# Relative-bias rows: 32 copies per head in eight stores and shifted loads in four pieces, in place of 128 copies in one store

## The reference

```
bucket = t5_bucket(max(t - s, 0))             # 32 buckets of distance
bias   = rel_bias[bucket]                     # [32 buckets, 8 heads]
logits = q . k * dh**-0.5 + bias              # s among the top-128 of query t, s <= t
probs  = softmax(logits);  out = probs @ v
```

## Time and profile before

| | us |
|---|---|
| median of three runs | 2206.12 (2200.85 to 2209.34) |
| profiled execution, whole | 2205.68 |
| its span, first to last instruction | 2204.0 |
| TensorE matmuls busy | 2006.9 (91%) |
| weight loads into TensorE busy | 1763.3 (80%) |
| GpSimd busy | 1047.3 (48%) |
| VectorE busy | 797.2 (36%) |
| ScalarE busy | 766.1 (35%) |
| mean granted TensorE clock | 0.961 |

### The profile page before, as it was taken

The page is one execution under the profiler, slowest core; times in us unless marked ns, Lnnn a source line. Parts: engine busy times, 40 slices in busy tenths (PEclk is TensorE's granted clock), DMA queues, the critical chain, the costliest instruction groups (busy, mean ns, idle before and its releaser), DMA issues.

```text
span 2204.0 us, 31094 instructions
## 1 busy us (share of the span) xinstructions
PE 2006.9 (91%) x12052; PEld 1763.3 (80%) x12052; DVE 797.2 (36%) x1298; ACT 766.1 (35%) x1198; POOL 1047.3 (48%) x573
## 2 busy tenths in 40 slices
PE   5999898999998969999997999999789993988997
PEld 5889898788888958877896888899668882756897
DVE  5536754444432055263623111010357700035212
ACT  3422332433321234345634333222433321335223
POOL 2634462766763444546446555533613440615552
PEclk9999999999999989999998999999899996998999
DMA  7655354466653213222121333322212334201132
GB/s 256 214 172 163 106 163 153 137 178 184 192 153 102 87 48 88 77 86 72 53 67 58 95 95 95 95 95 88 71 48 77 96 94 78 86 29 39 50 98 84
DMA packets 238064, 232.72 MB, mean 106 GB/s; under 512 B 15016, under 2 KB 219600, under 8 KB 237696
## 3 DMA queue, kind: packets, MB, share of 16 engines
q1 hardware_dynamic: 237448, 230.97, 34.6%
q10 hardware_dynamic: 504, 0.15, 0.0%
HBM read 226.33 MB, written 4.75 MB: 105 GB/s over the span
## 4 chain that ended last, share of the span: by engine, by line
PE 83%; DVE 6%; DMA 4%; ACT 3%; issue 1%; DVEq 1%; SPq 1%; POOL 1%; ACTq 0%
PE acc L1254 71%; PE ms L604 2%; PE acc L579 2%; DMA raw<-in_w_in 2%; DVE x_tok L1733 1%; PE ada_ps L1305 1%; PE aux L593 1%; PE aux L1254 1%; DMA x_tok<-in_x 1%; SPq L358 1%; DMA ada_raw<-in_kv_ada_w 1%; PE aux L1450 1%; DVEq L1735 1%; DVE ada_wide L1633 0%; DVE ada_acc L1655 0%
## 5 line engine op out<-in xcount | busy, mean ns | idle before, releaser
L708 POOL TENSOR_TENSOR w_lo<-raw,w_hi 128x1024 fp32r<-128x1024 f32 (+1 forms) x300 | 742.3, 2488 | 739.8 <-ACT w_hi L702 739.4
L1254 PE MATMUL acc<-hh,w_hi 128*128 128x512 f32 x1344 | 532.8, 396 | 44.5 <-ACT ogate L991 37.4
L1254 PE MATMUL acc<-hh,w_lo 128*128 128x512 f32 x1344 | 526.6, 392 | 0.0
L1254 PE MATMUL acc<-hl,w_hi 128*128 128x512 f32 x1344 | 526.5, 392 | 0.0
L702 ACT ACTIVATE w_hi<-raw 128x1024 fp32r<-128x1024 f32 (+1 forms) x300 | 308.8, 1040 | 437.2 <-DMA raw<-in_ffn_w_down 199.1
L1254 PEld LDWEIGHTS acc<-hh,w_hi 128*128 128x128 f32 x1344 | 254.9, 190 | 107.3 <-ACT ogate L991 37.8
L1254 PEld LDWEIGHTS acc<-hl,w_hi 128*128 128x128 f32 x1344 | 254.7, 190 | 53.8 <-issue 1.7
L1254 PEld LDWEIGHTS acc<-hh,w_lo 128*128 128x128 f32 x1344 | 254.2, 189 | 54.1
L1254 PE MATMUL acc<-w_hi,hh 128*128 128x256 f32 x704 | 200.7, 285 | 0.0
L1254 PE MATMUL acc<-w_hi,act_hi 128*128 128x256 f32 x704 | 200.6, 285 | 0.0
L1254 PE MATMUL acc<-w_lo,act_hi 128*128 128x256 f32 x704 | 199.3, 283 | 0.0
(11 more groups left out here) (370 smaller groups left out, 3053.2 us busy)
## 6 DMA issues: line engine op xcount, KB each, us to landing
raw<-in_ffn_w_gu SPq DMA_DIRECT2D x176, 256.0 KB, 3.2
ada_raw<-in_ada_w SPq DMA_DIRECT2D x80, 512.0 KB, 3.9
raw<-in_w_in SPq DMA_DIRECT2D x52, 512.0 KB, 3.6
raw<-in_ffn_w_down SPq DMA_DIRECT2D x40, 512.0 KB, 3.4
raw<-in_a_w_in SPq DMA_DIRECT2D x32, 512.0 KB, 4.9
raw<-in_a_w_out SPq DMA_DIRECT2D x16, 512.0 KB, 3.7
ada_raw<-in_kv_ada_w SPq DMA_DIRECT2D x16, 512.0 KB, 4.7
raw<-in_kv_w SPq DMA_DIRECT2D x16, 512.0 KB, 3.6
```

Source lines behind the costliest of these rows:

```text
L708: eng.tensor_tensor(w_lo[:, s, 0:nk, :], raw[:, s, 0:nk, :], w_hi[:, s, 0:nk, :].bitcast(F32), ALU.subtract).then_inc(w_split, 1)
L1254: ins = pe.matmul(out, w, x, start=first and n == 0, stop=last and n == len(pairs) - 1, skip_group_check=check)
```

## The change: what it does

The one store of 8 x 128 rows becomes eight stores, one for each head, of 32 copies each, all on the SP queue and on one semaphore. The load of a head's shifted tile becomes four loads of 32 partitions, at r = 0, 32, 64 and 96. The piece at r starts r places earlier in the row, so that its 32 partitions read copies 0 to 31. SP and ScalarE wait for eight completions of the stores, and GpSimd for four completions of the loads for a tile. ScalarE's wait is new and stands ahead of its first `decays`. The other attention keeps its one load for a tile. The DRAM tensor keeps its size; copies 32 to 127 are not written or read.

```diff
+REL_COPIES = 32
@@ tables of the two attentions
-        fx.update(..., toeplitz=False, qz_free=(f_ps, 1), mb_free=None)
-        dx.update(..., toeplitz=True, qz_free=(mt_ps, 1), mb_free=(m_s_ready, MH + 1))
+        fx.update(..., toeplitz=False, rb_dmas=1, qz_free=(f_ps, 1), mb_free=None)
+        dx.update(..., toeplitz=True, rb_dmas=P // REL_COPIES, qz_free=(mt_ps, 1), mb_free=(m_s_ready, MH + 1))
@@ attention_sp
-                    sp.dma_start(a["rb"][:, e, :], source(2 * i + e)).then_inc(a["rb_in"][e], 16)
+                    for rows, ap in source(2 * i + e):
+                        sp.dma_start(a["rb"][rows, e, :], ap).then_inc(a["rb_in"][e], 16)
@@ attention_pool
-                    pool.wait_ge(a["rb_in"][e], 16 * (i + 1))
+                    pool.wait_ge(a["rb_in"][e], 16 * a["rb_dmas"] * (i + 1))
@@ the SP queue, behind the loads of "mo"
             sp.wait_ge(row_u_ready, 1)
-            sp.dma_start(io["rel_u"], row_u[:].unsqueeze(1).broadcast_to([AH, P, UROW])).then_inc(rel_u_out, 16)
+            for h in range(AH):
+                sp.dma_start(io["rel_u"][h:h + 1, 0:REL_COPIES, :], row_u[h:h + 1, :].unsqueeze(1).broadcast_to([1, REL_COPIES, UROW])) \
+                    .then_inc(rel_u_out, 16)
...
-            sp.wait_ge(rel_u_out, 16)
+            sp.wait_ge(rel_u_out, 16 * AH)
...
-            attention_sp(sp, dx, lambda h: bass.AP(io["rel_u"].tensor, h * P * UROW + P - 1, [[UROW - 1, P], [1, T]]))
+            def shifted_rows(h):
+                return [(slice(r, r + REL_COPIES), bass.AP(io["rel_u"].tensor, h * P * UROW + P - 1 - r, [[UROW - 1, REL_COPIES], [1, T]]))
+                        for r in range(0, P, REL_COPIES)]
+            attention_sp(sp, dx, shifted_rows)
@@ ScalarE, ahead of the first decays
+            act.wait_ge(rel_u_out, 16 * AH)
             decays(0)
```

More of the change, by code:

```diff
@@ L330, in build_program @@
                 a[n] = sem(f"{kind}_{n}")
-        fx.update(q=q_fox, k=k_fox, v=v_fox, pairs=NH // 2, toeplitz=False, qz_free=(f_ps, 1), mb_free=None)
-        dx.update(q=aq, k=ak, v=av, pairs=AH // 2, toeplitz=True, qz_free=(mt_ps, 1), mb_free=(m_s_ready, MH + 1))
+        fx.update(q=q_fox, k=k_fox, v=v_fox, pairs=NH // 2, toeplitz=False, rb_dmas=1, qz_free=(f_ps, 1), mb_free=None)
+        dx.update(q=aq, k=ak, v=av, pairs=AH // 2, toeplitz=True, rb_dmas=P // REL_COPIES, qz_free=(mt_ps, 1), mb_free=(m_s_ready, MH + 1))
         block = ctx.enter_context(nc.Block())
@@ L777, in _ @@
             load_group(sp, "fox_out", 0, 0)
-            attention_sp(sp, fx, lambda h: io["fox_nd"][ds(h, 1), :].broadcast_to([P, T]))
+            attention_sp(sp, fx, lambda h: [(slice(0, P), io["fox_nd"][ds(h, 1), :].broadcast_to([P, T]))])
             load_stage(sp, "fox_out", skip=1)
```

## The result

| | before | after |
|---|---|---|
| median of the runs | 2204.79 us (4 runs, 2200.85 to 2209.34) | 2175.99 us (4 runs, 2172.62 to 2177.17) |
| profiled execution, whole | 2205.68 | 2176.71 |
| its span | 2204.0 | 2175.0 |

The ratio is 0.9861 with a 95% interval of 0.9842 to 0.9880: faster by 1.4%. A second series of the same kernel gave 0.9846 (0.9819 to 0.9872). The forecast was 2180.0 us.

The account below looks back on a forecast made before the run. The bias-row store filling the DMA queues was taken to hold up a weight load and TensorE. Store bytes falling from 51.4 to 25.7 us, other terms about 0, gave 2205.68 - 25.7 = 2180.0 us, range 2166 to 2188.

Parts of the forecast that it names:

- What bounds, and the deadline: DMA queues, filled by the bias-row store, keep TensorE idle 37.4 us; a weight unit landed by 1825.9 costs nothing.
- The store's time: Eight stores move 0.655 MB, one path at a time at 25.5 GB/s: 25.7 us where the old took 51.4.
- half or a quarter of that rate: One partition gives 12.8 GB/s: no change, 2205.5 us, chance 0.06; or 6.4: slower, 2257 us, chance 0.08.
- Eight issues in place of one: SP issues the stores in 2.6 to 6.7 us, hidden, or the next load starts up to 1.9 us later.
- The low clock: TensorE's clock falls 3.6 us into its idle time, back 4 us after restart; 2.0 us paid in both kernels.
- the second rival: The store is hidden whole, under 14.0 us, leaving 2.9 us of idle time: gain 36.5, time 2169.2 us, chance 0.24.
- The loads of `rb` and the waits: Tile loads cost 0, without cover 0.5 us; ScalarE's new wait ahead of `m_e` costs 0.0 to 0.1 us.
- Total: Whole kernel: 2205.68 - 25.7 = 2180.0 us, against the profiled execution, -1.2%.

Follow-up runs that it names:

- the order 0, 4, 1, 5 and on: The changed kernel with its eight stores in the order of heads 0, 4, 1, 5, 2, 6, 3, 7: 2171.32 us, ratio 0.9841.
- the spread rows: Bias rows on partitions 0, 4 to 28: the kernel before, one store of 128 copies, 2171.79 us; the changed kernel, eight stores, 2170.15 us.
- the kernel with one store of 32: The changed kernel with one store of 8 x 32 rows in place of eight stores of 32: 2170.07 us, ratio 0.9838.
- The best version: One store of 8 x 32 rows, and ScalarE splits the next units of `mz` ahead of its gate chain, against the changed kernel: 2165.49 us (2173.29 there).
- the loads alone: The changed kernel with the one store of 8 x 128 rows put back, tile loads still in four pieces: 2208.21 us, ratio 1.0006.

## Why the prediction was right, and where its steps were off

**What bounds, and the deadline.** Right. The wait was where it was said to be, and the restart again came 3.6 us behind the first landing (1840.58 - 1836.99).

**The store's time.** The mechanism was right: one path at a time, twice as slow for a byte as the old store. The rows of the trace before did not force that choice. It rested on 51 being twice 25.4, and the forecast said that nothing in the trace excluded half or a quarter of that rate; that it held was shown only by the runs. The size was off. The forecast had 25.7 us for the bytes and a landing 29.1 us behind the issue; it came at 25.6. In the trace's records of DMA packets the rows of 2560 bytes ran from 1813.62 to 1835.06, 21.4 us. Of the 4.3 us less, 1.9 are the rate (27.6 GB/s in place of 25.5: 23.8 us for 0.655 MB), and 2.4 are the overlap of heads 3 and 4, where the source passes from one group of partitions to the other, which the forecast left out. Against this, starting and the weight load behind the store took 4.1 us and not 3.4. It was 4.1 before the change too, since the old store's packets ran for 50.7 us and not the 51.4 that 51 GB/s gave. So TensorE waited 8.1 us in place of 11.7. The rate of 25.5 was taken from stores that use all paths.

The Trainium skill's figure of 27.2 GB/s for a port (*SBUF — State Buffer*, "Door 1: The DMA port swizzle") was the nearer one. Its grouping of partitions 0 to 3 and 4 to 7 agrees with the 47 GB/s where the source passes over, with the order 0, 4, 1, 5 and on, and with the spread rows. The Trainium skill's rule on the outermost dimension (*DMA: Bandwidth & Descriptors*, "Rules for kernel authors") agrees too: the share went from 0.47 to about 0.9. But more engines brought no bytes here.

**Eight issues in place of one.** Wrong. The forecast had 2.6 to 6.7 us; SP was held for 16.0 us, and the next weight load was issued at 1827.82, some 11 us after its turn (TensorE's use of the slot, at about 1816.3 with the 2.9 us shift). I had reasoned from the rows queued for an engine, 16 where there had been 128. I take it to have cost nothing, because the load's bytes would have stood behind the stores' in any case; no run separates the two. Nor did the issue of that load fall back to 0.4 us: it took 2.70.

**The low clock.** As forecast, it stayed: TensorE's clock (length, busy us, PEclk, DMA share, GB/s) fell here 2.6 us into the idle time, which began at 1832.5, and was back 4.7 us after the restart.

```profile
1834.00:1835.00 1.00, 0.00 (x0) 1.00 0.94 246
1835.00:1836.00 1.00, 0.00 (x0) 0.55 0.93 289
...
1844.00:1845.00 1.00, 1.00 (x4) 0.50 0.00 0
1845.00:1846.00 1.00, 1.00 (x5) 0.83 0.00 0
```

In the second rival I had a wait of 2.9 us pass without a fall, because the former one had come after 3.6 us. That was wrong. In the kernel with one store of 32 the same wait of 3.0 us (2.9 forecast) did bring the low clock. Its trace, TensorE alone, the wait from 1842.05 to 1845.08:

```profile
1843.00:1844.00 1.00, 0.00 (x0) 1.00 0.60 84
1844.00:1845.00 1.00, 0.00 (x0) 0.85 0.99 341
1845.00:1846.00 1.00, 0.92 (x2) 0.50 0.29 99
```

Of the 4.7 us that taking this wait away was worth, 3.0 are the wait and 1.7 the low clock. So the hidden store was worth 1.7 us less than the rival said, near 2171, and 2170.07 to 2171.79 were measured. The best version, which takes the wait away, wins the 1.7 us with it.

**The loads of `rb` and the waits.** Right that they cost nothing. GpSimd's first 20 adds took 20.42 us in place of 20.18. The run with the loads alone was at 1.0006, and ScalarE did not wait for a store in front of its first `m_e`. The +1.6 us of the attention in the profile after is not shown to be theirs: of the seven other profiles with the loads in pieces five took 57.8 to 58.5 us there, the same as the 58.5 of the two with one load, and two took 60.6. Nor is the -4.2 us the change's: the kernel with the loads alone, with the full old wait, took 123.3 us from the restart to the attention. The clock accounts for both. From the restart to the attention TensorE stood idle for 16.5 us in either profile, but was busy for 106.2 us at a mean granted clock of 0.93 where it had been busy for 110.5 at 0.90 (the loads alone: 106.8 at 0.93). In the attention it was the other way round: TensorE was busy for 53.4 us at 0.87 where it had been busy for 50.8 at 0.92. What moves the clock there from run to run is left open; no run was made for it. The 2.9 us ahead of the store lie within what other profiles show: the same `ogate` starts between 1818.7 and 1823.6 in them.

**Total.** TensorE waited 29.3 us less, the slow group took 0.5 us more (13.4 us for 12.9), and the rest is scatter that happens to cancel in these two profiles. That agrees with the medians, 28.8 us apart. The forecast gain of 25.7 us was thus 3 us short, and the missing part is in the store's time.

## What to carry to other kernels

Before a store is divided or spread over more engines, look at which partitions its source lies on: a broadcast out of a few neighbouring partitions is bound by them, and more engines don't help (51 GB/s from partitions 0 to 7, 205 from 0, 4, to 28, at about the same DMA share). A bulky transfer whose result is needed late still blocks every load queued behind it, so its price is read at the loads' deadline. And a wait of 3.0 us on TensorE cost 4.7 here, because the clock fell with it.

## What the runs showed of the hardware that I had not expected

One partition alone feeds a store with 27.6 GB/s, no less than the 25.5 that four partitions of a group gave together in the old store. A DMA share near 0.9 went with a rate of 27 GB/s, and one of 0.51 with 205: the share tells how long the engines hold packets, not how many bytes they move. And SP's issue of a small store waits for earlier ones: three went out in 2.1 us, then each took as long as one needs to drain (2.97 us), though an engine had only a few rows in its queue, while one store with 128 rows for an engine was issued in 0.84 us. What is counted there, the runs don't show.
